# Two-block model on one core: state-space head stage with scores in bank 7, output squares and sums one pair later, two of four states copied by VectorE, first out-projection weights cast ahead of the state copies

## The reference

```
cb = einsum('bclgn,bcsgn->bcgls', cm, bm)                      # scores, one per group of 4 heads
y_diag = einsum('bcgrls,bcsgrp->bclgrp', cb[:, :, :, None] * exp(seg), xd)
y_off = einsum('bcqgn,bcgrpn->bcqgrp', cm, h_in) * exp(a_cs)[..., None]
y = y_f + flip(y_b) + d_skip[:, None] * xs                     # forward and backward scan
y = y.reshape(b, l, D_SSD) * silu(z)
y = rmsnorm(y, norm_w)                                         # mean of squares over 1024 channels
x = x + g1 * (concatenate([y, fourier], -1) @ w_out)
x = x + g2 * hier_moe(modulate(rmsnorm(x, norm2), sh2, sc2), ...)   # 32 experts, 2 per token
```

## Time and profile before

| what | value |
|---|---|
| median of 3 runs | 1427.8 us (1423.75, 1427.8, 1427.95) |
| the profiled execution's own time | 1429.21 us |
| its span, first to last instruction | 1427.4 us |
| mean granted TensorE clock | 0.972 of 2.4 GHz |
| PE / DVE / ACT / POOL busy | 1308.0 / 794.8 / 610.0 / 88.7 us |
| moved by DMA | 383.32 MB, 269 GB/s over the span |
| head stage | about 886 to 939 us of the span |

### The profile page before, as it was taken

The page is one execution under the profiler, slowest core; times in us unless marked ns, Lnnn a source line. Parts: engine busy times, 40 slices in busy tenths (PEclk is TensorE's granted clock), DMA queues, the critical chain, the costliest instruction groups (busy, mean ns, idle before and its releaser), DMA issues.

```text
span 1427.4 us, 26314 instructions
## 1 busy us (share of the span) xinstructions
PE 1308.0 (92%) x11170; PEld 1108.6 (78%) x11170; DVE 794.8 (56%) x1220; ACT 610.0 (43%) x947; POOL 88.7 (6%) x69
## 2 busy tenths in 40 slices
PE   7999999999999999999999999899978777877777
PEld 7989698999989988999989999588544334444535
DVE  5558857877467587777458796874222111222214
ACT  6553346444456686454446654763211111121112
POOL 2000000300003100020000000410000000000000
PEclk9999999999999999999999999899998989899999
DMA  9655357554574567445562050468999999999996
GB/s 371 246 206 200 139 216 284 206 190 177 183 312 167 210 251 294 179 177 185 199 240 96 34 236 1 163 266 342 427 428 428 427 429 429 427 429 425 427 428 267
DMA packets 30359, 383.32 MB, mean 269 GB/s; under 512 B 3552, under 2 KB 3728, under 8 KB 7216
## 3 DMA queue, kind: packets, MB, share of 16 engines
q1 hardware_dynamic: 29504, 377.72, 65.2%
q0 software_dynamic: 752, 4.11, 0.7%
HBM read 380.77 MB, written 1.05 MB: 267 GB/s over the span
## 4 chain that ended last, share of the span: by engine, by line
PE 64%; DMA 24%; DVE 6%; ACT 4%; issue 1%; POOL 0%; SPq 0%; DVEq 0%; ACTq 0%; POOLq 0%
PE ps L699 63%; DMA ring<-in_experts 24%; DVE work L2023 2%; DVE w_lo L2011 2%; ACT w_hi L1463 1%; ACT work L1463 1%; ACT HM L1463 1%; DVE work L2011 1%; DVE HM L2011 0%; PE ps L858 0%; DVE SQ L2017 0%; DVE sg_lo L2011 0%; DVE small L2187 0%; DMA ring<-in_dense 0%; ACT L1463 0%
## 5 line engine op out<-in xcount | busy, mean ns | idle before, releaser
L2011 DVE TENSOR_TENSOR w_lo<-ring,w_hi 128x1024 fp32r<-128x1024 f32 (+1 forms) x273 | 338.2, 1245 | 202.9 <-ACT w_hi L1463 202.7
L1463 ACT ACTIVATE w_hi<-ring 128x1024 fp32r<-128x1024 f32 (+1 forms) x273 | 287.0, 1055 | 262.8 <-PE ps L699 258.9
L699 PE MATMUL ps<-in_hi,w_hi 128*128 128x256 f32 x1376 | 388.2, 282 | 11.2 <-DVE w_lo L2011 10.2
L699 PE MATMUL ps<-in_hi,w_lo 128*128 128x256 f32 x1376 | 385.1, 280 | 0.0
L699 PE MATMUL ps<-in_lo,w_hi 128*128 128x256 f32 x1376 | 385.1, 280 | 0.0
L699 PE MATMUL ps<-ring,work 128*32 128x256 f32 (+3 forms) x2520 | 206.0, 460 | 80.9 <-DMA ring<-in_experts 72.6
L699 PEld LDWEIGHTS ps<-in_hi,w_hi 128*128 128x128 f32 x1376 | 261.1, 190 | 15.6 <-issue 13.6
L699 PEld LDWEIGHTS ps<-in_lo,w_hi 128*128 128x128 f32 x1376 | 261.0, 190 | 0.2
L699 PEld LDWEIGHTS ps<-in_hi,w_lo 128*128 128x128 f32 x1376 | 261.1, 190 | 0.0
L699 PEld LDWEIGHTS ps<-ring,work 128*32 128x32 f32 (+1 forms) x2520 | 84.3, 118 | 185.4 <-issue 109.2
L2023 DVE SCALAR_TENSOR_TENSOR X<-ps,mod,X 128x256 f32<-128x256 f32 x136 | 59.0, 479 | 249.7 <-PE ps L699 249.6
(11 more groups left out here) (291 smaller groups left out, 1890.8 us busy)
## 6 DMA issues: line engine op xcount, KB each, us to landing
ring<-in_experts SPq DMA_DIRECT2D x89, 2048.0 KB, 23.1
ring<-in_dense SPq DMA_DIRECT2D x82, 2048.0 KB, 7.5
ring<-in_experts SPq DMA_DIRECT2D x5, 512.0 KB, 20.9
work<-in_experts SPq DMA_DIRECT2D x1, 2048.0 KB, 13.4
ring<-in_dense SPq DMA_DIRECT2D x3, 512.0 KB, 7.2
spare<-in_experts SPq DMA_DIRECT2D x1, 1536.0 KB, 10.6
cst<-in_ret_cst POOLq DMA_DIRECT2D x1, 1280.0 KB, 13.3
cst<-in_experts SPq DMA_DIRECT2D x1, 1280.0 KB, 5.6
```

What stands on the lines that cost most here:

```text
L699: i = pe.matmul(o, l, r, start=start, stop=stop)
L1463: x = act.activation(o, i, f, **kw)
L2011: i = dve.tensor_tensor(out=o, in0=x, in1=y, op=op)
```

## The change

It has four parts and a renaming.

- The score tiles leave the rotation: they are written to bank 7 and have semaphores of their own (`cb_full`, `cb_read`). The rotation has four tiles fewer, so all later tiles, those of the expert stage too, take other banks, and each waits for another tile: y3 for y1 instead of row 8, y2 for y0 instead of cb1, y5 for y3 instead of row 12, y6 for row 13 instead of y4, row n for row n - 4 from row 8 on (row 6 for state 3, row 7 for row 2), and y0 for state 2.
- ScalarE's squares of pairs 0 and 1 and of 2 and 3 move from the end of heads 7 and 11 to heads 8 and 12, behind their four Relu. TensorE's sums move from behind y3, y5 and y7 to behind y4 and y6, the third to the place of the fourth.
- ScalarE copies states 0 and 1, VectorE states 2 and 3, behind its first out-projection `w_lo`. y tile 0 waits for all four.
- ScalarE casts the first two out-projection chunks ahead of its state copies.
- `ones_set`, `csil_zero` and `pads_zero` become one semaphore `fills` that counts to 3.

```diff
@@ the order of tiles
-    else:
+    elif _kind != "cb":
         _seq.append((_kind, _i))
@@ TensorE
                 elif kind == "cb":
-                    t = TILE["cb", i]
-                    await_room(pe, t)
+                    if i:
+                        pe.wait_ge(s["cb_read"], i)
                     for j in range(2):
-                        mm(bank(t)[:, j * T:(j + 1) * T], b_lat[:, i, j * P:(j + 1) * P], c_lat[:, i, :], True, True,
-                           bank_full[t % ROT] if j == 1 else None)
+                        mm(ps[:, MODB, j * T:(j + 1) * T], b_lat[:, i, j * P:(j + 1) * P], c_lat[:, i, :], True, True,
+                           s["cb_full"] if j == 1 else None)
...
                     if i == 0:
                         pe.wait_ge(s["xd_ready"], 4)
-                        await_read(pe, TILE["state", 2])
-                        await_read(pe, TILE["state", 3])
+                        for g in range(SG_):
+                            await_read(pe, TILE["state", g])
...
-                    if i % 2 and i > 1:
-                        y_sums(i // 2 - 1)
+                    if i in (4, 6):
+                        y_sums(i // 2 - 2)
...
                 if b == KD:
+                    y_sums(2)
                     y_sums(3)
@@ ScalarE
                 if h == 2:
-                    for g in range(SG_):
+                    weights_hi(MIX0 + 2)
+                    for g in range(2):
                         read(TILE["state", g], h0[:, g, :])
-                    weights_hi(MIX0 + 2)
...
+                    if h >= 8 and h % 4 == 0:
+                        y_square(h // 4 - 2)
...
-                if h >= 7 and h % 4 == 3:
-                    y_square(h // 4 - 1)
+            y_square(2)
             load_norm_tables()
             y_square(3)
@@ VectorE
             def masked(g):
 
-                t = TILE["cb", g]
-                await_full(dve, t)
+                dve.wait_ge(s["cb_full"], g + 1)
...
-                bk, o = bank(t), cbx[:, g % 2]
+                bk, o = ps[:, MODB, :], cbx[:, g % 2]
...
-                tt(o[:, 1, P:384], bk[:, T:2 * T], smask[:, 1, P:384], MUL, bank_read[t % ROT])
+                tt(o[:, 1, P:384], bk[:, T:2 * T], smask[:, 1, P:384], MUL, s["cb_read"])
...
                 if h == 1:
                     weights_lo(MIX0 + 2)
+                    for g in range(2, SG_):
+                        t = TILE["state", g]
+                        await_full(dve, t)
+                        dve.tensor_copy(h0[:, g, :], bank(t)).then_inc(bank_read[t % ROT], 1)
```

More of the change, by code:

```diff
@@ L859, in turned @@
                 i.then_inc(bank_full[t % ROT], 1)
-            pe.wait_ge(s["ones_set"], 1)
+            pe.wait_ge(s["fills"], 1)
             next_input(0, "ret_g", ())
@@ L1585, in input_hi @@
                 act.wait_ge(s["in_lo_ready"], KD * (i + 1))
-            act.wait_ge(s["ones_set"], 1)
+            act.wait_ge(s["fills"], 1)
             fn(small[:, 501:502], ones[:, 0:1], ACT.Identity)
@@ L1590, in _ @@
             next_input(0, "ret_g", ())
-            act.wait_ge(s["csil_zero"], 1)
+            act.wait_ge(s["fills"], 2)
             fn(csil[:, :, 0:2], cut(col("c", 0, 2 * KD), KD, 2), ACT.Silu, s["csil_ready"])
@@ L1651, in _ @@
             next_input(2, "lru_u", (2,))
-            act.wait_ge(s["pads_zero"], 1)
+            act.wait_ge(s["fills"], 3)
             def first_tap(j):
@@ L2126, in gain_of @@
                 return lambda c: col("norm_g", i * KD + c)
-            dve.memset(ones[:, :], 1.0).then_inc(s["ones_set"], 1)
-            dve.memset(csil[:, :, :], 0.0).then_inc(s["csil_zero"], 1)
+            dve.memset(ones[:, :], 1.0).then_inc(s["fills"], 1)
+            dve.memset(csil[:, :, :], 0.0).then_inc(s["fills"], 1)
             dve.wait_ge(s["ld_gain"], 16)
@@ L2263, in _ @@
             next_input(2, "lru_u")
-            dve.memset(upad[:, :, 0:LPAD], 0.0).then_inc(s["pads_zero"], 1)
+            dve.memset(upad[:, :, 0:LPAD], 0.0).then_inc(s["fills"], 1)
             first, count = CHUNK_AT["lru_u"][0], CHUNK_AT["lru_u"][1] + CHUNK_AT["lru_y"][1]
@@ L2510, in _ @@
                 if h % 4 == 0:
-                    await_read(dve, TILE["cb", h // 4])
+                    dve.wait_ge(s["cb_read"], h // 4 + 1)
                 dve.wait_ge(s["dec_ready"], h + 1)
```

6 lines of the change are left out of this document (3 added, 3 removed).

## The result

The changed kernel takes **1432.64 us** in the median of 8 runs (1430.85 to 1436.86), the kernel before 1428.73 (8 runs, 1423.75 to 1431.29). The ratio on record is **1.0036, 95% interval 1.0023 to 1.0050**, which is +5.1 us (+3.3 to +7.1). The forecast was +0.7 and no change; the measured median lies just over the top of the range, on the side of rival 2.

A forecast was written before the change was run, and what follows sets the result against it. Full DMA engines bound the kernel, with the head stage setting when their stream starts. Terms +1.1 - 0.5 - 0.7 + 0.7 = +0.6, taken as +0.7, on 1427.8 gave 1428.5 us; range 1424.0 to 1432.5.

The forecast's parts named there:

- rival 2: y0's new wait drops the clock: y0 and cb1 at 1.2 GHz, 3.4 us more, up to 1432.4; chance 0.15.
- What bounds the kernel: DMA engines full from 995 us; the head stage's gain or loss reaches the end one for one.
- Rival 3: Slack at the weight stream's restart hides the 0.7 us, so the end does not move: 1427.8; chance 0.1.
- States and first out weights: Start of the head stage: y0 waits for VectorE's state copies, 2.1 us later, and y1 starts late; term +1.1.
- its records start 2.31 us after y0: Score tile cb1 behind y0: starts 2.31 us after y0, ends 1.13 later, full at 901.9.
- its product for head 3 is 1.1 late: VectorE waits 1.1 us for cb1, delaying head 3's product, so y1 starts at 904.0, not 902.90.
- Scores in a bank of their own, squares later: At y3: the wait for ScalarE's row 8 read goes, VectorE's product for head 7 is next late; term -0.5.
- -0.7 for cb3: First sum moved between y4 and cb3: cb3 comes 0.7 us earlier, about VectorE's wait; bounds 0 and -0.7.
- The last two y tiles: y6 to y7: second sum now ahead of y7's blocks, y7 at 937.25 instead of 936.51; term +0.7.
- The sums as a whole: TensorE's moved sums: -0.7 ahead of cb3, +0.7 ahead of y7, 0 for those behind y7.
- Rival 1: y1 and y3 keep the upper clock, gaining 1.6 and 2.2 us: -3.1 in all, 1424.7; chance 0.2.
- Rival 4: GpSimd's product meets w_lo and takes the inputs first, w_lo waits 1.27 us: +2.0, 1429.8; chance 0.1.

The follow-up runs named there:

- e3: The changed kernel with VectorE's two state copies ahead of its w_lo instead of behind it; ratio 1.0001 to the kernel before.
- e13: The changed kernel with extra unread matmuls ahead of y0 (4), y1 (2) and y3 (4); ratio 1.0022 to the kernel before.
- e5: The changed kernel with four extra unread matmuls ahead of all of y0's waits; ratio 1.0022 to the kernel before.
- e12: The kernel before with only the scores in bank 7, the squares later and the common semaphore; ratio 0.9986.
- e1: The changed kernel with its states part undone: ScalarE copies all four states ahead of its casts; ratio 1.0008 to the kernel before.
- e4: The changed kernel with four extra unread matmuls in front of y0, misplaced behind its wait for the bank; ratio 1.0030 to the kernel before.
- e10: The kernel before with only TensorE's three sums moved as in the change; ratio 1.0028.
- e16: The kernel before with only the first sum moved, from behind y3 to behind y4; ratio 1.0005.
- e14: The kernel before with the three sums moved, plus extra unread matmuls ahead of y1 (3), y3 (4) and y5 (2); ratio 0.9993.
- e6: The kernel before with extra unread matmuls ahead of y1 (three) and y3 (four); ratio 0.9991.
- e9: The changed kernel with VectorE's copies ahead of w_lo, sums at their old places, extra unread matmuls ahead of y1 (3), y2 (2), y3 (2); 0.9975 of before.
- e11: e7 plus two extra unread matmuls ahead of each of y1, y2 and y3; ratio 0.9975 to the kernel before.
- e2: The kernel before with the states part alone: casts first, VectorE copying two states behind w_lo, y0 waiting for all four; ratio 1.0023.
- e7: e12 plus ScalarE's first weight casts ahead of its four state copies; ratio 0.9985 to the kernel before.

## Why the prediction was wrong, point by point

- **What bounds the kernel: right.** The head stage moves the held loads and the end one for one: 7.9, 7.8 and 7.7 us in the profile, and 15 of the 17 other profiled executions keep the distance from load to end within 1.6 us. Rival 3 (it does not reach the end) is out.
- **"States and first out weights", +1.1: the step that failed first.** Its parts were right, 1.28 us of copies (taken: 1.4) and y0 at 898.70 (898.5). The step "its records start 2.31 us after y0" took y0 at the duration that it had without a wait; behind the wait of 2.16 us that the step itself had worked out, y0 took 4.5 and cb1 1.80. The step "its product for head 3 is 1.1 late" kept that product's duration as well; it grew from 0.96 to 1.27 us, and to 1.93 where the clock was held. The part costs 3.3 us alone and 4.0 as the last one added. e3 shows that all of it comes from y0's late start. Of the 4.5 us at y1 in the change, 2.4 are there with the clock held (e13) and 2.2 come with the lower clock. How the 3.3 to 4.0 us at the end divide is open; e5 and e13 have the clock at 1.00 in y0 and cb1 and are still at 1.0022.
- **Rival 2: right on mechanism and place, by luck on the number.** It put y1 4.5 us later (1.1 + 3.4), and 4.55 were measured; but the clock's share was too high and the order's too low. Its total, +4.1 to +4.6, meets the +5.1 although that holds 3 to 4 us for the sums and -2.0 for the bank, which rival 2 did not have. Its rows held two waits of 1.73 and 2.29 us that were followed by a clock of about 0.5, and the head stage held none of such a length that was not. The expert stage of the same trace did hold some (two rows are in the last section), so the rows made this rival likely, more than 0.15, but did not decide for it. Its "against", that the rows of heads 4 and 5 break the wait up, failed: they are done before the wait begins.
- **"Scores in a bank of their own, squares later", -0.5: the sign right, undersized, and in e12's profile not by its mechanism.** e12 measures -2.0; y3 gains 0.1 us counted from y0, and the rest comes behind it, from the clock. The rest of the term, -0.7 for cb3, belongs to the moved sum. It failed in the change, where VectorE waited 2.18 us for the fourth masked scores and the forecast had none. Where y4 kept the clock it came in e1 and e4 (no wait) and not in e10 and e16 (0.74).
- **"The last two y tiles", +0.7: right in size** (4.80 us between y6 and y7 for 4.03). **The sums as a whole, 0: the second step that failed.** They cost 4.0 us by themselves (2.0 to 6.0), 3.1 between e12 and e1. The step moved 1.0 us of work from one place to another and kept every other duration. In the profiles of the change and of e3 the sum is gone from behind y3, where TensorE's clock was low, and y4 runs low too. In the times e14 fits that, since with the clock held nothing measurable is left; that it is this one sum was not shown (e16: 1.0005).
- The three parts measured each against the kernel before are -2.0, +4.0 and +3.3 us, +5.3 together, against +5.1 for the change. They add up within their intervals, so no large interplay of the parts is left to explain.
- **Rival 1** (the clock stays up by itself) did not happen; the waits ahead of y1 and y3 are 1.36 and 1.91 us. **Rival 4** did not happen where it was looked for: GpSimd's product ran beside the copies, `w_lo` kept its 2.35 us. GpSimd after:

```profile
897.14 1.27 POOL L677 TENSOR_TENSOR cst<-act,work 128x512 f32<-128x512 f32 x1 [3.08 <-ACT act L1464]
```

- The text on the kernel before gives the state tiles eight matmuls each; they are four, in eight records. Nothing in the sum used it.
- Of the signs listed: the held loads came later and the end with them, but by 7.9 us instead of about 1; y7 started right behind its blocks; ScalarE did wait at the first square, 0.43 us, at 917.08, and not at the second; "a granted clock of 0.5 in y0" was the sign named for a wrong forecast.

## What to carry to other kernels

When a change puts a wait of a microsecond or more in front of a group of small matmuls, price the group behind it at both clocks and look in the whole trace, not only in the stage, for what followed such waits; and when it takes work away from behind a slow tile, ask whether that work ran while the clock was low. Price the rest of the delayed chain again as well: an instruction that starts later can meet another engine's (0.96 us became 1.93). Order by who is waited for: the same two copies cost nothing ahead of `w_lo` and 3 to 5 us behind it. To say what a changed clock explains, hold it in both kernels and compare these two. Where a wait can't be removed, matmuls that nobody reads, placed ahead of all waits, kept the clock up in the tiles right behind them in the profiles of all six kernels in which they stood so (e5, e6, e9, e11, e13, e14); a tile further on could fall still (y5 in e9 and e13).

## What the runs showed of the hardware

- The fall of the clock is not a function of the wait alone. It came after waits of 2.14 and 2.16 us (y0 of e2 and of the change), late in y0's first part in the one and from y0's start in the other, and after waits of 1.0 us (y3 of e7 and e12, 2.46 and 2.83 us for the first part); it did not come after waits of 1.08 and 1.28 us in e6 (y2, y5) nor after 2.33 us ahead of y3 in the profiled executions of e2 and e16. TensorE of e16, then two groups of one shape in the expert stage of the kernel before, each behind a wait of 2.88 us for a DMA:

```profile
914.88 1.52 PE L699 MATMUL ps<-HM,work 128*64 128x256 f32 x16 [2.33 <-ACT act L1463]
```
```profile
1335.18 1.92 PE L699 MATMUL ps<-ring,work 128*32 128x512 f32 x16 [2.88 <-DMA ring<-in_experts]
...
1360.66 3.45 PE L699 MATMUL ps<-ring,work 128*32 128x512 f32 x16 [2.88 <-DMA ring<-in_experts]
```

- TensorE: Matmul & The Clock Gate in the Trainium skill, in its section HAM oscillation, tells of waits for DMA between groups of matmuls that make the clock fall each time. This case agrees that waits between groups are followed by the lower clock, with waits on other engines too and down to 1.0 us: y3 of e12 took 2.83 us behind one of 1.01. It does not agree on each time: of two equal waits of 2.88 us for a DMA one was followed by 1.92 us, the other by 3.45. What decides, in a given execution, whether a wait of 1 to 2.9 us is followed by a fall is left open.
- One kernel can have times in groups: e10 with 1428.8 to 1429.0 (3) and 1432.4 to 1434.8 (4), e1 with 1427.7 to 1429.2 (4) and 1431.6 to 1433.5 (7), and nothing between. The kernel before shows it rarely: of 35 times taken beside e13 to e16, three are 1433.6 to 1434.7 and the rest at most 1431.1. A profile shows one execution and can be of either group. That the clock makes the groups was not shown execution by execution.
- Slow tiles take a little less than twice as long: from y0's start to the next group's it is 4.47 us in the change for 2.31 before, a factor of 1.94; cb1's is 1.73 for 1.06, 1.63. The records of a row tile's later matmuls are 0.41 us for 0.27.
- A VectorE product of two SBUF inputs (128x768) that is 0.94 to 0.96 us alone takes 1.27 to 1.93 when it starts during a GpSimd product of 1.27, and ends 0.81 to 0.83 us behind that product's end (the change, e2, e5, e13).
- VectorE's copy of 128x512 out of PSUM to SBUF is 0.678 us by itself in the change (two in 1.28, since one starts before the other's end); the statistics read of the same shape, from which the prediction priced it, was 0.684. ScalarE's two took 1.08.
